# Two-layer decoder trunk, second mixer: value blocks issued from SyncE's queue, the last value products one unit later

## The reference

```
attn = softmax(q1 k1 + bias) - lam * softmax(q2 k2 + bias)      # causal, 512 x 512
o    = attn @ v                                                # 512 x 128 per head
o    = rmsnorm(o, subln_g) * (1 - lambda_init)
out  = concat over heads(o) @ b_w_o                            # 512 x 1024
```

## Time and profile before

| | us |
|---|---|
| median of 3 runs | 1580.41 (1580.26 to 1580.99) |
| the profiled execution | 1581.12 |
| its span, first to last instruction | 1579.3 |
| PE busy | 1557.7 (99% of the span) |
| DVE busy | 930.8 (59%) |
| ACT busy | 585.7 (37%) |
| POOL busy | 502.3 (32%) |

### The profile page before, as it was taken

How to read it: one execution, slowest core, us unless ns; L and a number is a source line. 1 busy time by engine, 2 the same in 40 slices (tenths; PEclk the granted TensorE clock), 3 DMA queues, 4 the chain that set the end, 5 groups by cost and what they waited for, 6 DMA issues and landing times.

```text
span 1579.3 us, 22036 instructions
## 1 busy us (share of the span) xinstructions
PE 1557.7 (99%) x7890; PEld 1282.6 (81%) x7890; DVE 930.8 (59%) x1569; ACT 585.7 (37%) x1056; POOL 502.3 (32%) x900
## 2 busy tenths in 40 slices
PE   9999999999999999999999999999999999999998
PEld 7788888888888788888888878888778888888887
DVE  6466466567456854536355677778585453635565
ACT  5223324314324522212223445777452221312344
POOL 4067578488491200000001126888420000000111
PEclk9999999999999999999999999999999999999998
DMA  6565566465443233333333344454333333333331
GB/s 171 141 171 154 143 166 158 143 171 144 122 132 109 79 102 93 95 102 90 99 93 93 101 122 141 123 138 130 101 93 94 94 104 96 93 95 91 100 110 71
DMA packets 327204, 184.37 MB, mean 117 GB/s; under 512 B 44857, under 2 KB 312690, under 8 KB 327138
## 3 DMA queue, kind: packets, MB, share of 16 engines
q1 hardware_dynamic: 300112, 158.61, 35.3%
q0 software_dynamic: 26768, 24.88, 6.0%
q10 hardware_dynamic: 258, 0.04, 0.0%
HBM read 157.11 MB, written 10.60 MB: 106 GB/s over the span
## 4 chain that ended last, share of the span: by engine, by line
PE 81%; POOL 10%; DVE 2%; DMA 2%; SPq 2%; ACT 2%; issue 1%; POOLq 0%; ACTq 0%; DVEq 0%
PE unit_out L1757 22%; PE unit_out L1759 22%; PE unit_out L1758 22%; POOL probs L919 8%; POOL sumsq L956 1%; PE attn L2117 1%; PE unit_out L1922 1%; PE attn L1905 1%; SPq L763 1%; PE unit_out L1923 1%; PE unit_out L1924 1%; DMA w_raw<-in_a_w_qkv_dram 1%; DMA probs<-blocks 1%; DVE w_lo L1284 1%; PE misc L1757 1%
## 5 line engine op out<-in xcount | busy, mean ns | idle before, releaser
L1757 PE MATMUL unit_out<-act_hi,w_hi 128*128 128x512 f32 x1849 | 724.4, 392 | 2.4 <-DVE act_lo L1299 1.2
L1759 PE MATMUL unit_out<-act_hi,w_lo 128*128 128x512 f32 x1849 | 718.2, 388 | 0.0
L1758 PE MATMUL unit_out<-act_lo,w_hi 128*128 128x512 f32 x1849 | 718.0, 388 | 0.0
L976 ACT ACTIVATE w_hi<-w_raw 128x1024 fp32r<-128x1024 f32 (+3 forms) x256 | 271.2, 1059 | 505.8 <-PE unit_out L1759 412.3
L1757 PEld LDWEIGHTS unit_out<-act_hi,w_hi 128*128 128x128 f32 x1849 | 347.2, 188 | 78.6 <-DVE w_lo L1284 4.5
L1759 PEld LDWEIGHTS unit_out<-act_hi,w_lo 128*128 128x128 f32 x1849 | 347.2, 188 | 71.9
L1758 PEld LDWEIGHTS unit_out<-act_lo,w_hi 128*128 128x128 f32 x1849 | 347.4, 188 | 69.8 <-issue 0.2
L1284 DVE TENSOR_TENSOR w_lo<-w_raw,w_hi 128x1024 fp32r<-128x1024 f32 (+3 forms) x256 | 320.2, 1251 | 114.5 <-ACT w_hi L976 114.2
L956 POOL TENSOR_TENSOR sumsq<-sumsq,square 128x512 f32<-128x512 f32 x41 | 57.9, 1411 | 843.3 <-ACT square L1004 841.6
L919 POOL DMA_DIRECT2D probs<-blocks x448 | 221.3, 503 | 135.2 <-DVE blocks L1377 109.1
L928 POOL DMA_DIRECT2D heads<-probs_t x256 | 139.1, 552 | 67.4 <-DVE probs_t L1377 67.0
(11 more groups left out here) (316 smaller groups left out, 1399.8 us busy)
## 6 DMA issues: line engine op xcount, KB each, us to landing
w_raw<-in_w_ff_dram SPq DMA_DIRECT2D x128, 512.0 KB, 4.0
w_raw<-in_a_w_qkv_dram SPq DMA_DIRECT2D x56, 512.0 KB, 4.4
probs<-blocks POOLq DMA_DIRECT2D x448, 32.0 KB, 2.5
w_raw<-in_b_w_qkv_dram SPq DMA_DIRECT2D x24, 512.0 KB, 4.2
w_raw<-in_a_w_qkv_dram SPq DMA_DIRECT2D x32, 256.0 KB, 3.1
w_raw<-in_w_ple_gate_dram SPq DMA_DIRECT2D x16, 512.0 KB, 4.0
soft<-soft_blocks POOLq DMA_DIRECT2D x128, 40.0 KB, 1.9
heads<-probs_t POOLq DMA_DIRECT2D x256, 16.0 KB, 2.7
```

Source lines behind the costliest of these rows:

```text
L976: sc.activation(weights_of(u)[0][:, 0:width, :], w_raw[par][:, 0:width, :], ACT.Copy).then_inc(hi_done, 1)
L1757: te.matmul(bank, w_k[0], hi, start=start, stop=False)
L1758: te.matmul(bank, w_k[0], lo, start=False, stop=False)
L1759: return te.matmul(bank, w_k[1], hi, start=False, stop=stop)
```

## The change

POOL no longer issues the 16 DMAs of the values in the second mixer, only those of the probabilities. SP issues them, from its own queue and with a semaphore of their own, `values_b_landed`. For heads 0 to 5 they stand behind the load of the K unit two heads later, for head 6 behind the load of out unit 1, for head 7 behind the load of out unit 3. DVE, before it writes `probs_t` again, and PE, before the value products, wait for the new semaphore. The second part moves the value products of head 7 on PE: they stood ahead of the last chunk of out unit 4, and now stand behind out unit 5, ahead of out unit 6.

```diff
@@ block.sync
+            def spread_values_b(head):
+
+                sp.wait_ge(values_blocks, A_PAIRS + head + 1)
+                to = b_buf(head % 2, V).rearrange("p (t i q) -> p t i q", t=NT, i=NT)
+                of = probs_t[:, :].rearrange("p (j t q) -> p j t q", t=NT, j=NT)
+                for i, j in itertools.product(range(NT), range(NT)):
+                    sp.dma_start(to[j * SUB:(j + 1) * SUB, :, i, :], of[i * SUB:(i + 1) * SUB, j, :, :]
+                                 ).then_inc(values_b_landed, 16)
...
                 for n in range(KC):
                     load(At(first + n), view[:, 0:KC - late, n * P:(n + 1) * P])
+                    if layer and n in (1, 3):
+                        spread_values_b(B_HEADS - 2 + n // 2)
...
+                    if i == 1 and head > 1:
+                        spread_values_b(head - 2)
@@ block.gpsimd, spread_head
-                pool.wait_ge(values_blocks, A_PAIRS + head + 1)
-                spread_tiles(b_buf(head % 2, V), probs_t[:, :], NT, values_landed)
                 pool.wait_ge(soft_blocks_ready, head + 1)
                 spread_tiles(soft[:, 2, :], soft_blocks[:, :], B_TILES, soft_landed)
@@ block.vector, sub_b
-                    wait(ve, values_landed, (s + (A_PAIRS - 1)).times(16 * NT * NT))
+                    if s.reg is None and s.const == 1:
+                        ve.wait_ge(values_landed, A_PAIRS * 16 * NT * NT)
+                    wait(ve, values_b_landed, (s - 1).times(16 * NT * NT))
                     to_blocks(probs_t[:, :], b_v_t(1 - par)).then_inc(values_blocks, 1)
@@ block.tensor, values_b
-                wait(te, values_landed, (s + (A_PAIRS - 1)).times(16 * NT * NT))
+                wait(te, values_b_landed, (s - 1).times(16 * NT * NT))
@@ block.tensor, sub_b
                             out_early(e_unit, 1, (3, early - 1))
-                            values_b(s, par, has_scores)
+                            if has_scores:
+                                values_b(s, par, has_scores)
                             wait(te, o_ready, early + A_PAIRS)
                             out_early(e_unit, 1, (early - 1, early))
...
+                    if has_norm and not has_scores and i == 1:
+                        values_b(s, par, has_scores)
```

More of the change, by code:

```diff
@@ L609, in build @@
         values_landed = sem("values_landed")
+        values_b_landed = sem("values_b_landed")
         values_part = sem("values_part")
```

## The result

The changed kernel took 1582.8 us (median of 19 runs) where the kernel before, run beside it, took 1580.62. The ratio is 1.0015, 95% interval 1.0009 to 1.0022, so it is **slower by 2.4 us (1.4 to 3.5)**. The forecast was 0.85 us faster, called no difference. It is less than 0.2%, but clear of zero, and on the other side. All ratios here are of executions with a mean granted clock of 0.993 or more; one of the ten of e9_warm_late, 2616.57 us at a granted clock of 0.556, is not among them.

What follows compares the result with a forecast made beforehand. PE was taken as the bound, busy 1557.7 of 1579.3 us, so only its gaps could be won. Terms of -3.7, +0.4 and +2.45 sum to -0.85, from 1580.41 to 1579.6 us; range 1577.3 to 1583.0.

Steps and rivals of the forecast that it cites:

- step 1: On PE in the drain, the later place of head 7's value products was to win 3.7 us.
- Step 2: Head 7's chain behind the later products was to lengthen PE's wait at the late chunks, costing 0.4 us.
- Step 3: Head 7's sixteen DMAs in SP's queue were to delay out unit 4's load in the drain, costing 2.45 us.
- the pitch p: Time from issue to issue of the value DMAs on SP, between 0.41 and 0.75 us, taken as 0.55.
- d: ACT's lateness on out unit 4's weights, 16p - 5.8, put at 3.0 us; PE was to lose d less 0.55.
- 16p - 9.65: The whole change in kernel time as a function of the pitch p, put at -0.85 us.
- second rival: SP's queue backs up to a pitch of perhaps 1.0 us, giving 1586.8 us; 12 in 100.
- the case's own range: Kernel time of the forecast case for p of 0.475 to 0.65: 1578.4 to 1581.2 us.
- The stops of PE: In the drain PE was to wait near 1 us each at unit 4, head 6's turn and unit 5, 2.45 in sum.
- A quick SP: SP issues small DMAs quickly, p at most 0.41, giving 1577.3 us; 15 in 100.
- The clock: PE's three stops in the drain together lower its clock, 1.5 us come back, giving 1581.1 us; 15 in 100.
- The fourth rival: SP holds up each head and DVE waits before `probs_t`; no size, its chance counted within the second rival.

Runs made afterwards that it cites:

- e9_warm_late: The changed kernel plus 30 unused transposes on PE ahead of out unit 4: ratio 1.0014 to the kernel before.
- e1: The kernel before with only head 7's value products moved behind out unit 5, all value DMAs still on POOL: ratio 0.998, 3.2 us faster.
- e7: The kernel before plus 28 unused transposes on PE in the gap ahead of head 7's value products: ratio 0.9997.
- e8: e1 with DVE making unit 5's low weights ahead of head 6's low part: ratio 0.9978 to the kernel before, 3.5 us faster.
- e10: e8 without ACT's table load back to Exp in step 9 of the second mixer: ratio 0.9968 to the kernel before, 5.1 us faster.
- e4: The changed kernel with head 7's sixteen value DMAs back on POOL, heads 0 to 6 on SP: ratio 0.9983 to the kernel before, 2.7 us faster.
- e5: The changed kernel, head 7's sixteen DMAs moving one run of 512 bytes per partition, not four of 128 (timing only): 1583.83 us in one run.
- e2: The changed kernel with head 7's value products back at their old place, value DMAs on SP: ratio 1.0018 to the kernel before, 2.8 us slower.

## Why the prediction was wrong

**What bounds the kernel, and step 1: right.** The late place was put at -3.67 in the stretch up to unit 6, and e1 shows -3.67, with its wait of 0.40 at unit 5 where 0.5 was put. That the value DMAs didn't keep POOL from starting on head 7's probabilities was right too: it starts 1119.82 - 1109.96 = 9.86 us after head 6's products, and it was 1115.76 - 1105.90 = 9.86 before. But the conclusion that they don't land sooner was wrong by 1.2 us. Before, POOL stood still 1.22 us after three of the sixteen; with the change it doesn't:

```profile
1119.82 9.48 POOL L942 DMA_DIRECT2D soft<-soft_blocks  x16 [11.25 <-DVE soft_blocks L1389]
```

This gap is in all five traces that have every value DMA on POOL (before, e1, e7, e8, e10) and in none of the seven others, e4 among them, which has head 7's values on POOL. Why isn't shown. It doesn't reach the changed kernel's time, since the late place leaves the probabilities room.

**Step 2: right in kind and near in size.** The wait at the late chunks rose from 0.62 to 0.94, 0.32 where 0.4 was put. e10 shows its cause: with ACT's table load out of the chain it falls to 0.18, which says that this chain ends the wait.

**Step 3 failed, in one number: the pitch p.** It was taken as 0.55 from the bias loads, and the DMAs took 0.64 in general and, with the stall, 0.70 for head 7. The rest of the rule held. Unit 4's load landed in 4.0 us where 3.8 was put. With 0.70 the rule 16p - 5.8 gives d = 5.4. The trace has ACT start on unit 4's weights at 1126.80 - 1109.96 = 16.84 after head 6's products, where it was 1117.36 - 1105.90 = 11.46: also 5.4. Steps 1 and 3 then make -3.67 + 5.4 - 0.55 = +1.2, and the traces say 31.72 - 30.56 = 1.16. The sum 16p - 9.65 gives +1.6, inside the measured 1.4 to 3.5. At p = 0.60 its sign turns, and my value lay below that.

Part of this fit is luck. The ordinary pitch of 0.64 gives only +0.6, below the interval, and the rest up to +1.6 is the one stall, a term that the prediction had at nothing outside its second rival. The stall isn't peculiar to this execution: in e9, e5 and e2 ACT starts on unit 4's weights 16.92, 17.52 and 17.85 us after head 6's products, so d is 5.5, 6.1 and 6.4 there, where the ordinary pitch gives 16 x 0.64 - 5.8 = 4.4. That the time fell within the stated range is owed to its outer bound (p = 0.75); the case's own range reached only to p = 0.65.

What misled was the choice of the nearest row. I chose the median of 0.51 by the length of the runs, but e5 shows that run length makes no difference here. The bias expansions (L763, least 0.56, median 0.71) were nearer in value, and I had them only as the upper bound; by e5 their number of runs isn't the reason either. A better row stood in the trace of the kernel before and isn't among the rows. In the second mixer a weight load that finds SP idle takes 0.37, and the bias load straight behind it 0.58 (all eight of them 0.574 to 0.584):

```profile
959.43 0.37 SPq L731 DMA_DIRECT2D w_raw<-in_b_w_qkv_dram  x1
959.85 0.58 SPq L858 DMA_DIRECT2D bias<-bias_tiles_b  x1
```

With 0.04 to the next issue that is p = 0.62, and the sum is +0.3.

**The stops of PE.** I expected three of about 1 us (unit 4, turn, unit 5). There were two, 3.30 and 0.41. The turn didn't wait, since PE ran at 1.2 GHz ahead of it, after 3.30 us idle. The granted clock of that stretch (PE busy, PEld, DVE, ACT, POOL, clock, DMA share, GB/s), after:

```profile
1128.70:1131.50 2.80, 2.77 (x7) 2.22 (x8) 0.99 (x4) 2.75 (x5) 0.60 (x2) 0.50 0.63 172
```

**The rivals.** A quick SP is out: no value DMA took less than 0.59. A backed-up queue with a pitch near 1.0 is out as well, but it was right in its direction and in part in its mechanism (the stalls of 0.5 to 1.5 us), and the result lies between it and the forecast. The clock did fall, after one gap and not three, and by e9's trace it cost the changed kernel about 0.3 us, because ACT's chain was nearly as long. In e2, with a gap of 4.36 us, it is part of the 2.5 us lost, beside the load's own delay. How much is the clock's isn't separated. The fourth rival named a wait of VectorE for p above 0.6: head 0's lot took 0.65 each, and no wait shows, since these DMAs land in 2.1 us and not in the 2.7 that was put.

**Heads 0 to 6.** They were put at nothing. The trace has 0.3 us more over the six steps (e1, with no DMA moved, has 0.1 more), with a wait of 0.4 ahead of head 6's products, where it was 0.15 before. The DMAs of head 0 landed in time for VectorE, whose waits show none for them.

## What to carry to other kernels

A DMA that is moved to another queue is paid for by whatever load stands behind it there. Find that load, its spare time, and count the number of DMAs times the queue's pitch. Where the spare runs out, cutting the lot in two and letting a load through can do what taking it off the queue does (here 2.2 us won against 2.7, which the intervals can't tell apart). When the price decides the sign, work out the value at which the sign turns, and treat a nearest row that lies within a tenth of it as open. And the gains of two edits that touch the same gap can't be added: here one alone won 3.2 us and the other alone lost 2.8, and together they lost 2.4. The move to SP costs 2.8 where the old gap hides part of the late load, and 5.6 where the late place has already removed that gap.

## What the runs showed of the hardware that I had not expected

- On SP, sixteen DMAs of 32 partitions take the same time with one run of 512 bytes per partition (11.44 us) as with four of 128 (11.13 and 11.31 us). Within a lot one DMA may take 1.5 us (1.477 here), or the load behind it 2.09 (e2), and what they wait for is open.
- The time that SP is busy with an issue depends on what stands ahead of it. The load of an output unit takes 0.37 us when SP was idle (unit 3) and 0.59 straight behind the value DMAs (unit 4), both in the changed kernel.
- On POOL the same sixteen took 8.69 us in the kernel before (from 1106.78 on), 0.54 each. For these shapes the issue from SP is the slower one. From issue to landing they take 2.1 us (median) from SP where POOL's took 3.2 in the second mixer before; but POOL's lots of the same shape in the first mixer landed in 2.1 too. The 2.7 of the earlier trace rows is the median of both mixers. The Trainium skill ("DMA: Bandwidth & Descriptors", SWDGE vs HWDGE vs iDMA) holds the hardware path to be the one with the faster setup. The landing in the second mixer agrees with that, the landing in the first mixer and the time of the issuing engine don't.
- Freeing POOL didn't make it quicker to start. Its timeline and VectorE's at head 6, after:

```profile
1099.09 9.48 POOL L942 DMA_DIRECT2D soft<-soft_blocks  x16 [13.10 <-issue]
```

```profile
1096.05 1.51 DVE L1389 STREAM_TRANSPOSE soft_blocks<-soft 128x1280 f32<-128x1280 f32 x1
```

The blocks are ready at 1097.56 and the first DMA starts 1.5 us later, and so it was at head 3; at the six other heads it was 0.3 us. The probabilities are then issued by 1108.57, and PE waits 0.4 us for them. Why POOL starts late there is open.
